# First loads on one queue, modulation rows copied plainly, column sums of both halves at once, in a one-core transformer block kernel

## What is computed

```python
mod = jax.nn.silu(c) @ w_ada[l] + b_ada[l]                      # (1, 6 * 1024)
shift1, scale1, gate1, shift2, scale2, gate2 = jnp.split(mod, N_MOD, axis=-1)
h = modulate(rmsnorm(x, norm1_w[l]), shift1, scale1)            # h * (1 + scale) + shift
proj = h @ w_in[l]
...
x = x + gate1[:, None, :] * mix
h2 = modulate(rmsnorm(x, norm2_w[l]), shift2, scale2)
ffn = hierarchical_moe(h2, ...)                                  # 32 experts, top 2
x = x + gate2[:, None, :] * ffn
```

## Time and profile before

| | us |
|---|---|
| three runs | 918.87, 916.0, 918.78 |
| median | 918.78 |
| the profiled execution | 919.4 |
| its span, first to last instruction | 917.6 |
| TensorE busy in the span | 893.3 |
| VectorE busy | 410.6 |
| ScalarE busy | 314.3 |
| GpSimd busy | 106.2 |

### The profile page before, as it was taken

How to read it: one execution, slowest core, us unless ns; L and a number is a source line. 1 busy time by engine, 2 the same in 40 slices (tenths; PEclk the granted TensorE clock), 3 DMA queues, 4 the chain that set the end, 5 groups by cost and what they waited for, 6 DMA issues and landing times.

```text
span 917.6 us, 13421 instructions
## 1 busy us (share of the span) xinstructions
PE 893.3 (97%) x5530; PEld 575.9 (63%) x5530; DVE 410.6 (45%) x697; ACT 314.3 (34%) x507; POOL 106.2 (12%) x116
## 2 busy tenths in 40 slices
PE   5999999999999999999999999999998999999998
PEld 2688876777644434444344444444435899999886
DVE  2357725368522323222223232223234778888643
ACT  1227335342522222322222212222213555555531
POOL 1024463031000000000000000000000022222200
PEclk9999999999999999999999999999999999999999
DMA  9962259787999899999999999999999665555301
GB/s 353 415 291 93 93 193 355 282 326 292 398 402 419 313 420 421 421 419 420 420 421 418 419 421 420 423 419 419 421 421 357 217 194 183 180 179 184 128 1 47
DMA packets 60892, 289.47 MB, mean 315 GB/s; under 512 B 4500, under 2 KB 28692, under 8 KB 33688
## 3 DMA queue, kind: packets, MB, share of 16 engines
q1 hardware_dynamic: 59104, 284.13, 78.3%
q10 hardware_dynamic: 1720, 4.40, 1.2%
HBM read 287.47 MB, written 1.05 MB: 314 GB/s over the span
## 4 chain that ended last, share of the span: by engine, by line
PE 90%; DVE 3%; DMA 3%; issue 2%; ACT 1%; POOL 1%; SPq 0%; ACTq 0%; DVEq 0%
PE ps L1032 24%; PE ps L1056 12%; PE ps L537 8%; PE ps L1020 7%; PE ps L1153 7%; PE ps L1154 7%; PE ps L1155 7%; PE ps L620 4%; PE ps L1072 3%; PE ps L1045 2%; DMA ring<-in_ada_units_dram 2%; PE ps L552 2%; PE ps L520 2%; DMA S<-in_first_cols_dram 1%; PE ps L511 1%
## 5 line engine op out<-in xcount | busy, mean ns | idle before, releaser
L1035 PE MATMUL ps<-ring,proj 128*64 128x512 f32 x320 | 140.9, 593 | 0.0
L1032 PE MATMUL ps<-ring,proj 128*64 128x512 f32 x304 | 133.9, 593 | 0.0
L1853 DVE TENSOR_TENSOR w_l<-ring,w_h 128x2048 fp32r<-128x2048 f32 x33 | 75.5, 2292 | 44.8 <-ACT w_h L2201 44.8
L1153 PE MATMUL ps<-h_h,w_h 128*128 128x256 f32 x336 | 95.1, 283 | 0.0
L1154 PE MATMUL ps<-h_l,w_h 128*128 128x256 f32 x336 | 95.1, 283 | 0.0
L1155 PE MATMUL ps<-h_h,w_l 128*128 128x256 f32 x336 | 95.1, 283 | 0.0
L1032 PEld LDWEIGHTS ps<-ring,proj 128*64 128x64 f32 x304 | 41.1, 137 | 84.6 <-issue 84.6
L1032 PE MATMUL ps<-arena,proj 128*64 128x512 f32 x208 | 91.6, 593 | 0.0
L2201 ACT CAST w_h<-ring 128x2048 fp32r<-128x2048 f32 x33 | 62.8, 1903 | 81.4 <-PE ps L1155 76.9
L1709 DVE SCALAR_TENSOR_TENSOR RQ<-ps,gate_of,proj 128x512 f32<-128x512 f32 x32 | 24.0, 751 | 147.1 <-PE ps L1057 147.1
L2157 ACT CAST MX_r<-RQ 64x512 fp32r<-64x512 f32 x62 | 38.2, 616 | 143.9 <-DVE RQ L1709 143.1
(11 more groups left out here) (372 smaller groups left out, 1601.7 us busy)
## 6 DMA issues: line engine op xcount, KB each, us to landing
ring<-in_w_dram SPq DMA_DIRECT2D x114, 1024.0 KB, 15.0
arena<-in_w_dram SPq DMA_DIRECT2D x72, 1024.0 KB, 15.7
ring<-in_ada_units_dram SPq DMA_DIRECT2D x11, 2048.0 KB, 8.6
ring<-in_ffn_w_in_dram SPq DMA_DIRECT2D x22, 1024.0 KB, 8.1
ring<-in_in_units_dram SPq DMA_DIRECT2D x6, 2048.0 KB, 23.1
ring<-in_ffn_w_out_dram SPq DMA_DIRECT2D x5, 2048.0 KB, 8.0
arena<-in_in_units_dram SPq DMA_DIRECT2D x2, 2048.0 KB, 24.8
ring<-in_out_units_dram SPq DMA_DIRECT2D x2, 2048.0 KB, 9.2
```

The lines of the kernel that those rows point to most:

```text
L1032: pe.matmul(ps[0:SLOTS, :], XTe[i % 2][:, k, :], u1[:, k, :], start=(k == 0), stop=(k == 7))
L1035: t = pe.matmul(ps[64:64 + SLOTS, :], XTe[i % 2][:, k, :], u3[:, k, :], start=(k == 0), stop=(k == 7))
L1153: pe.matmul(ps, ah, bh, start=first, stop=False)
L1853: ve.tensor_tensor(low, src, dst.bitcast(F32), ALU.subtract).then_inc(split_ready, 1)
```

## The change

Four edits. The loads of `first_cols` and `C` are issued by SP ahead of `ada` 0, X behind it, and SP's wait for `first_cols` is gone; ScalarE issues none of the three. The view `by_eights` takes element c of each eight in place (a step of eight elements), and the copies of units 0 to 3 and 6 to 9 write plainly. `column_totals` (segments 3 and 4) waits for both halves and makes eight products with 128 columns of weights in place of sixteen with 64. One `turn_over(2)` ahead of `ada(3)` is gone.

```diff
-        by_eights = part_[:, :, :].rearrange("k a b -> k (a b)").rearrange("k (c p) -> k c p", c=8)
+        by_eights = part_[:, :, :].rearrange("k a b -> k (a b)").rearrange("k (p c) -> k c p", c=8)
...
             def column_totals(seg):
-                column_total(seg, 1, column_total(seg, 0))
+                ps = take("columns", seg)
+                for half in range(2):
+                    pe.wait_ge(*drained("ada", 2 * seg + half))
+                for c in range(8):
+                    i = pe.matmul(ps[:, 2 * c:2 * c + 2], by_eights[:, c, :], sel[:, 0:2], start=True, stop=True)
+                i.then_inc(*mm.up("columns", seg, 0))
+                mm.at["columns", seg, 1] = mm.n
...
             second = column_total(1, 0)
-            turn_over(2)
             ada(3, ada_half)
...
-                ve.tensor_copy(by_eights[:, :, 64 * (j % 2):64 * (j % 2) + 64].rearrange("k c p -> k p c"),
-                               full("ada", j)[:, :].rearrange("k (p c) -> k p c", c=8)).then_inc(*free("ada", j))
+                ve.tensor_copy(part[j % 2], full("ada", j)[:, :]).then_inc(*free("ada", j))
...
-            ac.dma_start(C[:, :], I["consts"][:, 0:258]).then_inc(const_in, 16)
-            ac.dma_start(first_cols, I["first_cols"]).then_inc(first_in, 16)
-            ac.dma_start(X[:, :, :], I["x"].rearrange("b (n p) d -> p (b n) d", p=128)).then_inc(x_in, 16)
-
...
-                if j in (6, 7, 8, 9):
-
-                    half = slice(64 * (j % 2), 64 * (j % 2) + 64)
-                    ac.copy(by_eights[:, :, half].rearrange("k c p -> k p c"),
-                            ps[:, :].rearrange("k (p c) -> k p c", c=8)).then_inc(*free("ada", j))
-                else:
-                    ac.copy(dst, ps[:, :]).then_inc(*free("ada", j))
+                ac.copy(dst, ps[:, :]).then_inc(*free("ada", j))
...
+            sp.dma_start(first_cols, I["first_cols"]).then_inc(first_in, 16)
+            sp.dma_start(C[:, :], I["consts"][:, 0:258]).then_inc(const_in, 16)
             load_ada(0)
-            sp.wait_ge(first_in, 16)
+            sp.dma_start(X[:, :, :], I["x"].rearrange("b (n p) d -> p (b n) d", p=128)).then_inc(x_in, 16)
             load_ada(1)
             load_ada(2)
```

## The result

The change makes the kernel slower: 926.84 us median of 5 runs (924.93 to 928.72) against 918.87 for the kernel before (5 runs), ratio 1.009 with a 95% interval of 1.0064 to 1.0117. That is 8 us more, where 1.9 less were forecast. The profiled execution has a span of 925.0, 7.4 more than the one before.

A forecast was written before the change was run, and what follows sets the result against it. TensorE, busy 97% of the span, was taken as the bound, its start set by the first 30 us of transfers. Loads -1.45, plain copy -0.34 and column sums -0.1 made -1.9: 918.78 to 916.9, range 914.5 to 920.2.

The forecast's parts named there:

- The strided weights: Column sums reading by_eights at a step of eight: no extra cost in the sum; dearer loads only as a rival, chance 0.1.
- the first rival: 48 weight loads on the path, each 53 ns longer at a step of eight: +2.5, giving 919.4; chance 0.1.
- My second rival: TensorE stays at the low clock to the end of the loads: +3.5 in all, 920.4; chance 0.1.
- The loads: Head: ada 1 queued early, so each landing from then on comes 1.45 us earlier, through to the first projection.
- The instruction fetch: Queue q8's fetch stays at ada 3's load; rival that it misses: 1.1 more gained, 915.8, chance 0.1.
- The plain copy: VectorE's copy into part on the head's path takes 0.69 in place of 1.05: -0.34 us.
- The merged sums: column_totals for segments 3 and 4 with 16 instructions of 128 columns, 1.62 to 1.78 each: -0.1 for both.
- The turn-over that goes: Four matmuls, 1.13 us at 27.54 ahead of ada 3, stand in a wait for its second half: 0.
- The bound on measurement: Whole kernel: measurements can't tell less than about 0.3%, 2.8 us, from no change; within that, chance 0.69.

The follow-up runs named there:

- the probe: Kernel before plus unread groups of products on X (64 or 128 columns, steps 1 to 16) and transposes, behind the head; no total time given.
- the loads alone: Kernel before with only first_cols, C, ada 0, X and ada 1 issued by SP in this order with no wait: 916.27, ratio 0.9991.
- both fillings: Changed kernel, scattered copies restored, turn_over(10) at the start, six more turn-overs behind ada 0's column sums: 917.36, ratio 1.0001; also with step-two weights: 916.27, 0.9988.
- the doubled sums: Kernel before with the sixteen products of each column_totals made twice, weights side by side: 923.61, ratio 1.0069.
- the layout alone: Kernel before with only plain copies and column-sum weights read at a step of eight, two halves of 64 columns kept: 928.71, ratio 1.0115.

## Why the prediction was wrong

**The strided weights**, the step that failed. It was the first rival, with a chance of 0.1 and +0.6 us. Both are wrong. In the sum the step stands at nothing: the column sums on the path keep their 1.1, and the two `column_totals` get -0.1 together, bounded by a row of transposes. Measured are +0.95 for each sum in the head and +1.8 for each `column_totals`. The chance: I took transposes (0.89 against 0.87 for eight) for evidence on ordinary products; the probe has 1.79 against 1.75 for the one and 2.97 against 1.49 for the other. The same rows had weight loads of 193 against 140 ns, and I explained them away. The Trainium skill, SBUF — State Buffer, section Door 1: The DMA port swizzle, says that each line of 16 bytes needs two hits for full bandwidth. The probe agrees, with 1.53 at a step of two and 2.96 at four. The same passage counts four float32 elements as the stride that is free; measured, a step of four already pays the whole price, and it says nothing of transposes, which pay next to nothing (1.79 against 1.75). I had that rule and gave it to a rival.

The size: 53 ns for 48 loads, 2.5 us. Measured are (2.01 - 1.06) / 16 = 59 ns for 64 columns and (3.57 - 1.68) / 16 = 118 ns for 128, so 1.9 and not 0.85 for each `column_totals`. The Trainium skill, TensorE: Matmul & The Clock Gate, section LDWEIGHTS, which the prediction cites, gives 107 ns for 128 columns as an estimate. That makes 1.71 for 16, which is 0.04 under the 1.75 of before, where the prediction has +0.04 and an argument against the change; at the step of eight the changed kernel has 223 ns. And the sums on the path were three in the head, not one: I counted by the chain of before, in which loads hide the first two. Once each sum takes 1 us more, TensorE is what is late, and all three count.

**The low clock.** My second rival had it at the end of the loads, through idle time. It did come in the head, granted 0.51 from 18.2 and 0.50 from 35.2 on, where it stretched six turn-over instructions from 1.49 to 2.59. But at 35.2 TensorE had worked without a gap since 17.59. What I missed is that it comes without any idle time, in mid-run too, at the longer stretches of narrow products. The two in mid-run are 2.9 us of the 7.4 between the profiled executions, and neither the sum nor a rival had them.

**The loads.** The stream is right in kind and mis-sized: `ada` 1 lands 0.9 earlier where I had 1.45. The pace was right, 4.9 behind X, but X itself lands at 12.6 in place of 12.07: half a us is lost at the start, which I had put at 0. Wrong is that the gain goes through to the projection. With the loads alone TensorE works from 17.48 on with hardly a gap but for the copies, `ada` 1 at the low clock takes 1.4 more, and the projection begins 0.1 later than before. The 0.9 us in the medians, whose interval touches no change, is not shown to come from the stream.

**The instruction fetch.** I left it at `ada` 3 and gave 0.1 to its missing that load. It did miss: it stands in the changed kernel at 27.5, past `ada` 3, whose second half landed 2.3 earlier, and `dn` 1 was late instead and gained only 0.7. Eleven other traces have a load late near the fetch too. Where the fetch comes at 21.2 or 21.6 (both fillings), `ada` 2 takes 6.4 in place of 4.9. Where it comes between 24.6 and 26.3 (six kernels), the second half of `ada` 3 takes 3.7 to 4.0 in place of 2.4. Where it comes between 27.2 and 27.9 (four), `dn` 1 takes 5.8 to 6.5 in place of 4.9. Two traces differ: in the probe, with the fetch at 25.6, the half of `ada` 3 takes only 3.0, and with the doubled sums, at 27.1, `dn` 1 takes only 5.2. So that the fetch holds the load fits most traces, but no run moves it alone, and its price isn't fixed. What sets its time stays open.

**The plain copy** is at 0.69, as forecast. That saved nothing here, since turn-overs of 1.06 stand beside the copy and TensorE was late. **The merged sums** cost 1.68 with weights side by side (1.62 to 1.78 forecast). **The turn-over that goes** was put at 0 because it stood in a wait. That holds for the chain of before; once the loads are earlier it stands on the path, and without it the projection begins 0.91 earlier (33.86 against 34.77). **The bound on measurement** of 0.3% was right too; runs of the kernel before lie from 914.7 to 920.6, and their times go with the mean granted clock: at 1.0 they take 914.7 to 916.2, at 0.994 some 920.0.

## What to carry to other kernels

When a change moves a scattered access from one side to the other, price the other side by a row of the same kind of instruction; a transpose's weight load says nothing about a product's. For float32, two elements of each 16-byte line were enough on both sides here, so look for the layout that gives both sides two before trading one for the other. And count the sums in the chain again after pricing: what hides behind loads before is on the path as soon as the engine is late.

## What the runs showed of the hardware

Weights of ordinary float32 products: 62 to 64 ns an instruction for 64 columns at a step of 1 or 2 elements, 114 to 124 at 4, 8 and 16; 113 to 122 against 208 to 229 for 128 columns. Transposes: 109 to 119 at steps of 1, 2, 8 and 16. Writes from VectorE and ScalarE at a step of 512 bytes: 1.04 and 1.05 us against 0.69 and 0.59 in a row, and 0.69 and 0.61 in runs of two. Of the stretches of products with two columns on the right in mid-run, all six of some 3.5 us or more (the changed kernel, the layout alone, the doubled sums, two each) had the granted clock fall to 0.5, between 2.1 and 4.0 us after their start, and none of the eighteen of 1.7 to 1.8 us did, in the nine kernels that have them there. Between the two lies the probe: a fall at 2.92 and 2.71 us with 128 columns of weights, none at 2.7 to 3.0 us with 64. In twelve of fourteen traces one load near the one instruction fetch of the head lands 0.9 to 1.6 us later than the stream's pace, in the other two 0.3 and 0.5; that the fetch is the cause isn't shown.
